# Identity and norm vectors loaded ahead of x, three chunks of x turned ahead of the first q tile, first two V quads queued among the q tiles

## The chip, the cores and the metric

The kernel runs on one core of a Trainium2 chip, written directly for its engines: TensorE (PE) multiplies and transposes, VectorE (DVE), ScalarE (ACT) and GpSimd (POOL) work on what it leaves, SyncE (SP) issues all the DMAs. Each engine runs its own list of instructions in order and waits on semaphores. The metric is the device time of one execution in microseconds, lower is better; the median of several runs is compared.

## The reference

One inference step of a one-layer decoder, all in float32. Prompt: 256 tokens; sample: 8 sequences of 4 new tokens, each with 2048 past tokens in a paged K/V pool (pages of 128 tokens).

```
h = rmsnorm(x, norm1_g)                      # x: 256 + 32 rows of 2048
q, k, v, u = split(h @ w_in)                 # w_in: 2048 x 4096
a = moba_attention(q, k, v, cache_k, cache_v, page_table)  # 8 heads of 128, top 3 blocks of 256
p = pool_mixer(u, hist)                      # causal means over 2, 4, 8, 16 tokens, then w_pool
x = x + concat(a, p) @ w_out
h2 = rmsnorm(x, norm2_g)
x = x + (silu(h2 @ w_gate) * (h2 @ w_up)) @ w_down         # width 5632
y = rmsnorm(x, norm_f_g)
```

Outputs are y, the new K and V rows and the pooling history.

## The kernel before

All 288 rows of x are held transposed: xT is 16 chunks of 128 features by 288 tokens. To come near float32 accuracy with the faster matmul format, every weight and every activation is split into a high and a low part. ACT writes the high part (w_hi at L576, hh at L579), DVE the low part (w_lo at L838, hl at L843), and PE adds three products (L1412, L1413, L1414).

**Weights** come as tiles of 128 x 1024 floats (512 KB). SP's `load` (L405) puts a tile into one of four raw slots; from the fifth on it first waits until PE has used the tile four before it. ACT makes w_hi, DVE w_lo in place, PE's `w_tile` (L1403) uses it. The first 16 tiles give q (q tiles 0 to 15: four 128-column blocks by two chunks by three products, 24 matmuls each), the next 48 (kvu tiles) give u, v and k.

**Start.** SP issues the tables (identity, ones, masks and biases, one DMA of 641 KB), x (two of 1 MB, one of 256 KB), four vectors (norm gains and pool scale) into `vec`, the page table, then q tiles 0 to 3 and `hist` (L397 to L460). PE waits for the tables and all four vectors, turns `vec` into gains (L1423), waits for x, and turns the chunks of x, each with three transposes (`x_turned`, L1426; helper `turn`, L1418) into one of three PSUM banks. DVE copies each chunk out (`x_taken`, L867, copy at L869). X_AHEAD = 6 chunks are turned and copied before anything else; then for each q tile j of the first eight PE turns chunks 2j + 6 and 2j + 7, waits until hl of chunks 2j and 2j + 1 is there, and does the tile. ACT (L604) and DVE (L884) follow the same order: two hh, one w_hi, two squares; two hl, one w_lo, two copies. Before q tile 8 PE adds the squares with `ones` from the tables (`sum_sq`, L1434) and waits for the mean.

**SP's order among the q tiles** (L457 to L465): the load of tile k, for k = 6 to 13 one K page after it (eight pages, the first two quads of K). Then kvu tiles 0 to 3, then load_v(0) and load_v(1), each four pages of V of 512 KB into one of two V buffers (L432), then kvu tiles 4 and 5, then the loop over the 32 quads: four K pages, four V pages, two or so kvu tiles a step. A page's number is read from `pages` into a register (L419) before its DMA is issued (L423 for K, L441 for V). load_v(0) waits until all of x and hist are transposed, as the V buffers lie over xs, vec and hist. load_v(n) from n = 2 waits until PE has used quad n - 2.

**After the q tiles** DVE turns the first K quad (L880) between w_lo of q tile 15 and w_lo of kvu tile 0. PE does kvu tiles 0 and 1, replicates q (L1470), then alternates K logits (L1525), kvu tiles and V products (L1507). V quad 0 is first read there in the second sequence's turn, near 147 us. Then come prompt attention, w_out, and from about 640 us the feed-forward loop.

Of the kernel before, what the change touches and what calls it, by code (L numbers as in the profile page):

```python
# [29 lines left out]
P = 128  # L30
# [38 lines left out]

OA_ORDER = (2, 3, 0, 1)  # L70
NORM2_ORDER = tuple(range(8, 16)) + tuple(range(8))
X_AHEAD = 6

K_BLOCKS = [(a, b) for b in range(T // 32) for a in range(4)]

# [74 lines left out]
def tile_at(k, i=0, per=0):  # L150

    if k < T_FF:
        return k, k // RAW, k % RAW, k % HI
    m = k - T_FF
    s = m % RAW_FF
    earlier = T_FF // RAW if s < RAW else 0
    return k + per * i, earlier + m // RAW_FF + (per // RAW_FF) * i, s, k % HI
# [12 lines left out]
def step_program(nc, A, O, at):  # L170
    ctx = ExitStack()
    with ctx:
        def sem(name):
            return ctx.enter_context(nc.semaphore(name))

        def sb(name, shape, dt=F32, stack=None):
            return (stack or ctx).enter_context(nc.sbuf_tensor(name, shape, dt))


        tab = sb("tab", [P, at["rel"][0]])  # L180
# [39 lines left out]
        rel = ext[:, :, :, :].rearrange("p c b i -> p (c b i)")[:, 0:384]  # L220
# [36 lines left out]
        vec = sb("vec", [56, P], stack=pre)  # L257
# [50 lines left out]
        tab_in, x_in, vec_in, pages_in = sem("tab_in"), sem("x_in"), sem("vec_in"), sem("pages_in")  # L308
# [46 lines left out]
        def final_step(n):  # L355
            part = n // 4
            return part, n % 4, P if part < 2 else TS
# [36 lines left out]
        @block.sync  # L394
        def _(sp):
            xp, xsam = A["x_prompt"][0], A["x_sample"].rearrange("b q d -> (b q) d")
            sp.dma_start(tab[:, :], A["tables"][:, 0:at["rel"][0]]).then_inc(tab_in, 16)  # L397
            for n in range(2):
                sp.dma_start(xs[:, n, :], xp[n * P:(n + 1) * P, :]).then_inc(x_in, 16)
            sp.dma_start(xs[0:TS, 2, :], xsam).then_inc(x_in, 16)  # L400
            for n, name in enumerate(("norm1_g", "norm2_g", "norm_f_g", "pool_scale")):
                g = A[name] if name == "norm_f_g" else A[name][0]
                sp.dma_start(vec[16 * n:min(16 * n + 16, 56), :], g.rearrange("(c p) -> c p", p=P)).then_inc(vec_in, 16)

            def load(t, src, free=True):  # L405

                _, _, s, _ = t
                if free:
                    sp.wait_ge(w_used, slot_free(t))
                k, w = src.shape[0] // P, src.shape[1]  # L410
                sp.dma_start(w_raw[:, s, 0:k * w].rearrange("p (k n) -> p k n", k=k),  # L411
                             src.rearrange("(k p) n -> p k n", p=P)).then_inc(w_in_s[s], 16)
# [4 lines left out]
            def page(pool, b, n):  # L417
                e = NPAGES * b + n
                idx = sp.value_load(pages[0:1, bass.ds(e, 1)], min_val=0, max_val=pool.shape[0] - 1)  # L419
                return pool[bass.ds(idx, 1), :, :].rearrange("a t n -> (a t) n")  # L420

            def load_k_page(n, g):
                sp.dma_start(kpage[:, n % 2, g, :], page(ck, n // NQUADS, 4 * (n % NQUADS) + g)  # L423
                             ).then_inc(k_in[n % 2][g], 16)
# [7 lines left out]
            def load_v(n):  # L432

                if n >= 2:
                    sp.wait_ge(v_done, n - 1)
                elif n == 0:

                    sp.wait_ge(xT_in, KC)
                    sp.wait_ge(hist_T, 2)
                for g in range(4):  # L440
                    sp.dma_start(vpage[:, n % 2, g, :], page(cv, n // NQUADS, 4 * (n % NQUADS) + g)  # L441
                                 ).then_inc(v_in[n % 2], 16)
# [9 lines left out]
            def load_kvu(n):  # L452
                m, r = n // 4, n % 4
                c0 = 4 * AW - CW * (m + 1)
                load(tile_at(T_KVU + n), w_in_d[512 * r:512 * r + 512, c0:c0 + CW])

            for k in range(16):  # L457
                c, j = k // 8, k % 8
                if k == 4:
                    sp.dma_start(hist[:, :], A["state_pool"][0].rearrange("b i c -> (b i) c")).then_inc(hist_in, 16)  # L460
                load(tile_at(T_Q + k), w_in_d[256 * j:256 * j + 256, 512 * c:512 * c + 512], free=k >= RAW)
                if k == 6:
                    sp.wait_ge(pages_in, 16)
                if 6 <= k < 14:
                    load_k_page((k - 6) // 4, (k - 6) % 4)  # L465
            for k in range(4):
                load_kvu(k)
            load_v(0)
            load_v(1)
            load_kvu(4)  # L470
            load_kvu(5)
            kp, vp = O["k_prompt"][0, 0].rearrange("t h d -> t (h d)"), O["v_prompt"][0, 0]
# [358 lines left out]
        def _(dve):  # L831
# [3 lines left out]
            def lo(t):  # L835
                n, _, s, u = t
                dve.wait_ge(hi_ready, n + 1)
                V.tensor_tensor(w_lo[:, s, :], w_raw[:, s, :], w_hi[:, u, :].bitcast(F32),  # L838
                                ALU.subtract).then_inc(lo_ready, 1)
# [27 lines left out]
            def x_taken(c):  # L867
                dve.wait_ge(xT_in, c + 1)
                V.tensor_copy(xT[:, c, :], XB[c % 3][:, 0:T]).then_inc(x_ready, 1)  # L869
# [11 lines left out]

            for c in range(X_AHEAD):
                x_taken(c)
            for j in range(8):  # L884
                for c in (2 * j, 2 * j + 1):
                    gained_lo(0, c, c)
                lo(tile_at(j))
                for c in (2 * j + X_AHEAD, 2 * j + X_AHEAD + 1):
                    if c < KC:
# [510 lines left out]
        def _(pe):  # L1400
            PE = nc.tensor

            def w_tile(t, width, chunks, banks, xh, xl, start, stop):  # L1403

                n, _, s, u = t
                pe.wait_ge(lo_ready, n + 1)
                for m, out in enumerate(banks):
                    for i, c in enumerate(chunks):
                        a = width * i + P * m
                        wh, wl = w_hi[:, u, a:a + P], w_lo[:, s, a:a + P]  # L1410
                        o = out[:, 0:T]
                        PE.matmul(o, wh, xh[:, c, :], start=start and i == 0, stop=False)  # L1412
                        PE.matmul(o, wh, xl[:, c, :], start=False, stop=False)  # L1413
                        last = PE.matmul(o, wl, xh[:, c, :], start=False, stop=stop and i == len(chunks) - 1)  # L1414
                last.then_inc(w_used, 1)

            def turn(out, in_, rows):
                return PE.transpose(out, in_, ident[0:rows, 0:rows])  # L1418
# [7 lines left out]
            def x_turned(c):  # L1426
                if c >= 3:
                    pe.wait_ge(x_ready, c - 2)
                for n in range(3):
                    rows = P if n < 2 else TS  # L1430
                    last = turn(XB[c % 3][:, P * n:P * n + rows], xs[0:rows, n, P * c:P * c + P], rows)
                last.then_inc(xT_in, 1)

            def sum_sq(stage):  # L1434
                pe.wait_ge(sq_added, KC * stage + KC)
                PE.matmul(bank[7][:, 0:T], ones, ssq[:, :], start=True, stop=True).then_inc(sq_summed, 1)

            for c in range(X_AHEAD):
                x_turned(c)

            for k in range(16):
                c, j = k // 8, k % 8
                if c == 0:
                    for n in (2 * j + X_AHEAD, 2 * j + X_AHEAD + 1):
                        if n < KC:
                            x_turned(n)
                    pe.wait_ge(h_ready, 2 * j + 2)
                if k in (2, 5):

                    n = k // 5  # L1450
                    pe.wait_ge(hist_in, 16)
                    pe.wait_ge(*((gains_ready, 1), (ext_ready, 1))[n])
                    for m in range(4):
                        last = turn(bank[6][:, 120 * m:120 * m + 120], hist[:, 512 * n + P * m:512 * n + P * m + P],
                                    NB * HIST)
                    last.then_inc(hist_T, 1)
                if k == 8:

                    pe.wait_ge(ext_ready, 2)
                    sum_sq(0)  # L1460
                    pe.wait_ge(ms_ready, 1)
                w_tile(tile_at(k), 512, (2 * j, 2 * j + 1), bank[4 * c:4 * c + 4], hh, hl, j == 0, j == 7)
# [278 lines left out]
            for k in range(16):  # L1741
                c, j = k // 4, k % 4
# [12 lines left out]
            for j in range(8):  # L1755
                pe.wait_ge(h_ready, KC + 2 * j + 2)
                c = NORM2_ORDER[2 * j]
# [36 lines left out]
            for n in range(12):  # L1794
                part, c, rows = final_step(n)
# [42 lines left out]
```

## Time and profile before

| | |
|---|---|
| median of 3 runs | 1486.53 us (1486.39 to 1490.85) |
| profiled execution, its own time | 1484.65 us |
| its span, first to last instruction | 1482.9 us |
| PE busy | 1400.8 us (94%) |
| DVE busy | 902.4 us (61%) |
| ACT busy | 501.9 us (34%) |
| HBM read | 328.10 MB, 225 GB/s over the span |
| mean granted TensorE clock | 0.986 of full |

Times in the trace are microseconds from the first instruction. "Busy" of PE counts the time in which a matmul is in flight, so its matmuls overlap and their durations are about twice their pitch. SPq, PEq and so on are the engines' queues, where DMAs are issued. A bracket such as "[1.32 <-DVE ms L848]" tells how long the engine stood before it and whose result ended the wait.

### The profile page before, as it was taken

Reading aid. Unit: us, or ns where it says so; the run is one execution under the profiler, and the core shown is the slowest. Engines: PE = TensorE matmul, PEld = TensorE weight load, DVE = VectorE, ACT = ScalarE, POOL = GpSimd, SP = SyncE. Lnnn points to the kernel's source line nnn. Section 1 sums busy time; section 2 is a strip of 40 time slices with the busy share of each in tenths; the row PEclk is TensorE's granted clock in tenths of the full one; section 3 lists DMA queues with packets and bytes.
Section 4 is the critical chain, followed back from the end, with each engine's and each line's share of the span. In section 5 each row is a group of like instructions: output and inputs, shape, how many; then the busy total and the mean of one; then the engine's idle time right before and its main releaser. Section 6 shows DMA issues by size and latency. Waiting matters only on the chain.

```text
span 1482.9 us, 34088 instructions
## 1 busy us (share of the span) xinstructions
PE 1400.8 (94%) x13894; PEld 1298.0 (88%) x13894; DVE 902.4 (61%) x1352; ACT 501.9 (34%) x663; POOL 109.3 (7%) x184
## 2 busy tenths in 40 slices
PE   6998999998688999999999999999999999999986
PEld 5987777776455789999999999999999999999986
DVE  4678777767666645787554555545554646464635
ACT  4322122112123333544343434343333333333333
POOL 2127500000001000200000000000000000000003
PEclk9999999999899999999999999999999999999998
DMA  5798999999999665655555555555555555555531
GB/s 187 257 327 292 371 401 400 399 399 392 404 369 328 219 205 177 199 158 192 175 162 168 168 160 166 170 164 162 169 166 161 168 169 160 166 170 164 164 126 65
DMA packets 164280, 334.41 MB, mean 226 GB/s; under 512 B 10223, under 2 KB 54440, under 8 KB 163599
## 3 DMA queue, kind: packets, MB, share of 16 engines
q1 hardware_dynamic: 164183, 333.06, 66.3%
q8 instruction: 68, 1.11, 0.3%
q14 instruction: 29, 0.24, 0.0%
HBM read 328.10 MB, written 5.27 MB: 225 GB/s over the span
## 4 chain that ended last, share of the span: by engine, by line
PE 78%; SPq 9%; DVE 5%; DMA 3%; issue 3%; ACT 1%; POOL 0%; POOLq 0%; ACTq 0%; DVEq 0%
PE banks L1412 23%; PE banks L1413 23%; PE banks L1414 23%; PE banks L1525 3%; SPq L419 3%; SPq L423 3%; SPq L441 2%; DVE kpage L880 2%; PE banks L1507 2%; DMA vpage<-in_cache_v 2%; PE banks L1418 2%; SPq L411 1%; DMA vec<-in_pool_scale 1%; DMA w_raw<-in_w_out 1%; PE banks L1591 0%
## 5 line engine op out<-in xcount | busy, mean ns | idle before, releaser
L838 DVE TENSOR_TENSOR w_lo<-w_raw,w_hi 128x1024 fp32r<-128x1024 f32 x360 | 440.3, 1229 | 416.2 <-ACT w_hi L576 415.2
L1412 PE MATMUL banks<-hh,w_hi 128*128 128x288 f32 x2176 | 645.7, 297 | 5.3 <-DVE w_lo L838 1.5
L1413 PE MATMUL banks<-hl,w_hi 128*128 128x288 f32 x2176 | 644.3, 296 | 0.0
L1414 PE MATMUL banks<-hh,w_lo 128*128 128x288 f32 x2176 | 642.0, 295 | 0.8 <-issue 0.8
L576 ACT ACTIVATE w_hi<-w_raw 128x1024 fp32r<-128x1024 f32 x360 | 378.9, 1058 | 687.1 <-PE banks L1414 462.2
L1412 PEld LDWEIGHTS banks<-hh,w_hi 128*128 128x128 f32 x2176 | 410.3, 189 | 23.4 <-issue 17.3
L1413 PEld LDWEIGHTS banks<-hl,w_hi 128*128 128x128 f32 x2176 | 410.5, 189 | 1.1 <-issue 1.0
L1414 PEld LDWEIGHTS banks<-hh,w_lo 128*128 128x128 f32 x2176 | 409.5, 188 | 0.6 <-issue 0.6
L1412 PE MATMUL banks<-ah,w_hi 128*128 128x288 f32 x704 | 208.8, 297 | 9.5 <-DVE af L1252 5.4
L1414 PE MATMUL banks<-ah,w_lo 128*128 128x288 f32 x704 | 209.5, 298 | 0.0
L1413 PE MATMUL banks<-al,w_hi 128*128 128x288 f32 x704 | 209.2, 297 | 0.0
L880 DVE STREAM_TRANSPOSE kpage<-kpage 128x1024 f32<-128x1024 f32 x128 | 150.1, 1217 | 13.5 <-DMA kpage<-in_cache_k 12.9
L1412 PEld LDWEIGHTS banks<-ah,w_hi 128*128 128x128 f32 x704 | 134.4, 191 | 10.0 <-issue 5.6
L1413 PEld LDWEIGHTS banks<-al,w_hi 128*128 128x128 f32 x704 | 134.4, 191 | 0.0
L1414 PEld LDWEIGHTS banks<-ah,w_lo 128*128 128x128 f32 x704 | 134.0, 190 | 0.0
L1525 PE MATMUL banks<-kpage,qr 32*32 32x256 f32 x4096 | 94.5, 407 | 17.3 <-DVE kpage L880 13.1
L1525 PEld LDWEIGHTS banks<-kpage,qr 32*32 32x32 f32 x4096 | 60.9, 106 | 45.2 <-DVE kpage L880 17.6
L1507 PE MATMUL banks<-vpage,pT 128*32 128x512 f32 x512 | 65.1, 621 | 12.8 <-DMA vpage<-in_cache_v 11.3
L1344 POOL COPY ssq<-sq 128x288 f32<-128x288 f32 x3 | 1.7, 551 | 939.2 <-ACT sq L593 939.2
L1207 DVE TENSOR_TENSOR xT<-xT,banks 128x288 f32<-128x288 f32 x176 | 67.8, 447 | 0.0
L1507 PEld LDWEIGHTS banks<-vpage,pT 128*32 128x32 f32 x512 | 17.3, 142 | 43.1 <-issue 29.9
L1347 POOL TENSOR_TENSOR ssq<-ssq,sq 128x288 f32<-128x288 f32 x45 | 43.2, 960 | 53.4 <-ACT sq L593 48.8
(193 smaller groups left out, 646.4 us busy)
## 6 DMA issues: line engine op xcount, KB each, us to landing
kpage<-in_cache_k SPq DMA_DIRECT2D x128, 512.0 KB, 7.9
vpage<-in_cache_v SPq DMA_DIRECT2D x128, 512.0 KB, 7.0
w_raw<-in_w_gate SPq DMA_DIRECT2D x88, 512.0 KB, 3.6
w_raw<-in_w_up SPq DMA_DIRECT2D x88, 512.0 KB, 3.6
w_raw<-in_w_down SPq DMA_DIRECT2D x88, 512.0 KB, 3.6
w_raw<-in_w_in SPq DMA_DIRECT2D x64, 512.0 KB, 9.7
w_raw<-in_w_out SPq DMA_DIRECT2D x32, 512.0 KB, 4.0
xs<-in_x_prompt SPq DMA_DIRECT2D x2, 1024.0 KB, 7.4
```

Of the source, the lines that this page charges most:

```text
L419: idx = sp.value_load(pages[0:1, bass.ds(e, 1)], min_val=0, max_val=pool.shape[0] - 1)
L423: sp.dma_start(kpage[:, n % 2, g, :], page(ck, n // NQUADS, 4 * (n % NQUADS) + g)).then_inc(k_in[n % 2][g], 16)
L576: return nc.scalar.activation(out, in_, ACT.Copy)
L838: V.tensor_tensor(w_lo[:, s, :], w_raw[:, s, :], w_hi[:, u, :].bitcast(F32), ALU.subtract).then_inc(lo_ready, 1)
L880: V.transpose(kpage[:, n % 2, g, :], kpage[:, n % 2, g, :]).then_inc(k_turned, 1)
L1207: ins = V.tensor_tensor(xT[:, m0 + m, :], xT[:, m0 + m, :], bank[4 * quad + m][:, 0:T], ALU.add)
L1347: G.tensor_tensor(ssq[:, :], ssq[:, :], sq[:, c % 2, :], ALU.add).then_inc(sq_added, 1)
L1412: PE.matmul(o, wh, xh[:, c, :], start=start and i == 0, stop=False)
L1413: PE.matmul(o, wh, xl[:, c, :], start=False, stop=False)
L1414: last = PE.matmul(o, wl, xh[:, c, :], start=False, stop=stop and i == len(chunks) - 1)
L1507: last = PE.matmul(OB[x][32 * g:32 * g + 32, :], pT[:, g, bass.ds(j, 32, 4)], vpage[:, n % 2, g, 512 * x:512 * x + 512], start=j == 0, sto ...
L1525: last = PE.matmul(S[32 * x:32 * x + 32, a, :], qr[32 * a:32 * a + 32, at_:at_ + 32], keys, start=j == 0 and c == 0, stop=j == NQUADS - 1 ...
```

## The change

The tables are loaded in two pieces: the identity alone first, the rest after the load of q tile 1, with its own count on the same semaphore, for which PE waits before q tile 8. The four vectors are issued right after the identity, before x. X_AHEAD goes from 6 to 3 for PE and DVE; PE then turns chunks 2j + 3 and 2j + 4 before q tile j, for j to 6, and DVE copies them after w_lo of tile j. load_v(0) moves to behind the load and K page of k = 11, load_v(1) to behind those of k = 13.

```diff
-X_AHEAD = 6
+X_AHEAD = 3
...
-            sp.dma_start(tab[:, :], A["tables"][:, 0:at["rel"][0]]).then_inc(tab_in, 16)
+            sp.dma_start(tab[:, 0:P], A["tables"][:, 0:P]).then_inc(tab_in, 16)
+            for n, name in enumerate(("norm1_g", "norm2_g", "norm_f_g", "pool_scale")):
+                g = A[name] if name == "norm_f_g" else A[name][0]
+                sp.dma_start(vec[16 * n:min(16 * n + 16, 56), :], g.rearrange("(c p) -> c p", p=P)).then_inc(vec_in, 16)
             for n in range(2):
                 sp.dma_start(xs[:, n, :], xp[n * P:(n + 1) * P, :]).then_inc(x_in, 16)
             sp.dma_start(xs[0:TS, 2, :], xsam).then_inc(x_in, 16)
-            for n, name in enumerate(("norm1_g", "norm2_g", "norm_f_g", "pool_scale")):
-                g = A[name] if name == "norm_f_g" else A[name][0]
-                sp.dma_start(vec[16 * n:min(16 * n + 16, 56), :], g.rearrange("(c p) -> c p", p=P)).then_inc(vec_in, 16)
...
             for k in range(16):
                 c, j = k // 8, k % 8
+                if k == 2:
+                    sp.dma_start(tab[:, P:at["rel"][0]], A["tables"][:, P:at["rel"][0]]).then_inc(tab_in, 16)
                 if k == 4:
                     sp.dma_start(hist[:, :], A["state_pool"][0].rearrange("b i c -> (b i) c")).then_inc(hist_in, 16)
                 load(tile_at(T_Q + k), w_in_d[256 * j:256 * j + 256, 512 * c:512 * c + 512], free=k >= RAW)
...
                 if 6 <= k < 14:
                     load_k_page((k - 6) // 4, (k - 6) % 4)
+                if k in (11, 13):
+                    load_v((k - 11) // 2)
             for k in range(4):
                 load_kvu(k)
-            load_v(0)
-            load_v(1)
             load_kvu(4)
             load_kvu(5)
...
                 if k == 8:
 
                     pe.wait_ge(ext_ready, 2)
+                    pe.wait_ge(tab_in, 32)
                     sum_sq(0)
                     pe.wait_ge(ms_ready, 1)
```

## Rows read from the trace of the kernel before

**Rows 1.** The page, part 4: the chain that ended last, by engine.
```profile
PE 78%; SPq 9%; DVE 5%; DMA 3%; issue 3%; ACT 1%; POOL 0%; POOLq 0%; ACTq 0%; DVEq 0%
```

**Rows 2.** Windows: stretch, us, PE, PEld, DVE, ACT, POOL busy, PEclk, DMA share, GB/s.
```profile
55.00:70.00 15.00, 14.38 (x109) 14.39 (x109) 10.47 (x15) 4.87 (x7) 0.00 (x0) 1.00 0.78 264
70.00:82.00 12.00, 12.00 (x93) 12.00 (x92) 9.71 (x10) 4.31 (x5) 0.00 (x0) 1.00 0.54 170
...
100.00:120.00 20.00, 19.57 (x389) 17.08 (x388) 15.57 (x16) 5.32 (x6) 17.08 (x37) 1.00 1.02 369
120.00:155.00 35.00, 30.41 (x535) 25.37 (x518) 33.56 (x53) 8.83 (x10) 27.50 (x59) 1.00 0.80 273
155.00:400.00 245.00, 218.99 (x3682) 168.18 (x3680) 173.65 (x270) 43.08 (x56) 13.28 (x31) 0.98 1.04 400
```

**Rows 3.** The chain of waits from 0 to 60: start us, us, what.
```profile
4.25 8.15 DMA vec<-in_pool_scale
...
12.53 5.50 PE banks L1418 x19
18.05 0.46 DVE xT L869
...
19.90 1.15 DVE w_lo L838
...
24.40 0.24 PE banks L1412
...
25.26 0.14 PE banks L1414
...
47.46 5.39 DMA w_raw<-in_w_in
```

**Rows 4.** The tile xs (x as loaded), its DMAs.
```profile
DMA to landing us min/median/max: 6.1/8.6/9.7
```

**Rows 5.** Timeline from 0: start us, us, engine, line, operation.
```profile
2.12 0.66 SPq L400 DMA_DIRECT2D xs<-in_x_sample  x1
2.82 0.92 SPq L403 DMA_DIRECT2D vec<-in_norm_g  x2
...
14.36 1.28 ACT L579 ACT_TABLE_LOAD   x1 [14.36 <-DVE xT L869]
```

**Rows 6.** Timeline of SP's queue, 52 to 99.
```profile
53.84 0.37 SPq L411 DMA_DIRECT2D w_raw<-in_w_in  x1
...
59.08 0.37 SPq L411 DMA_DIRECT2D w_raw<-in_w_in  x1
...
82.51 8.08 SPq L441 DMA_DIRECT2D vpage<-in_cache_v  x8
90.64 0.99 SPq L411 DMA_DIRECT2D w_raw<-in_w_in  x2
```

**Rows 7.** Timeline of ACT: w_hi of q tile 11 and of kvu tile 4.
```profile
58.47 1.06 ACT L576 ACTIVATE w_hi<-w_raw 128x1024 fp32r<-128x1024 f32 x1 [1.48 <-DMA w_raw<-in_w_in]
...
98.95 1.06 ACT L576 ACTIVATE w_hi<-w_raw 128x1024 fp32r<-128x1024 f32 x1 [12.86 <-DMA w_raw<-in_w_in]
```

**Rows 8.** Timeline of DVE: w_lo of q tile 15, K turns, w_lo of kvu tiles 0, 1.
```profile
73.51 1.23 DVE L838 TENSOR_TENSOR w_lo<-w_raw,w_hi 128x1024 fp32r<-128x1024 f32 x1 [1.25 <-ACT w_hi L576]
74.65 4.62 DVE L880 STREAM_TRANSPOSE kpage<-kpage 128x1024 f32<-128x1024 f32 x4
79.19 2.32 DVE L838 TENSOR_TENSOR w_lo<-w_raw,w_hi 128x1024 fp32r<-128x1024 f32 x2
```

**Rows 9.** Timeline of PE: q tile 8's first matmul, and replicate_q.
```profile
55.62 0.40 PE L1412 MATMUL banks<-hh,w_hi 128*128 128x288 f32 x1 [1.32 <-DVE ms L848]
...
87.45 1.89 PE L1470 MATMUL banks<-z,sq 128*128 128x256 f32 x8
```

**Rows 10.** A long PE pause: windows as rows 2, then the timeline row that ends it.
```profile
380.00:383.00 3.00, 0.00 (x0) 0.00 (x0) 2.86 (x11) 0.00 (x0) 0.00 (x0) 1.00 1.03 414
383.00:386.00 3.00, 0.00 (x0) 0.00 (x0) 3.00 (x4) 0.00 (x0) 0.00 (x0) 0.52 1.02 419
...
386.31 3.65 PE L1507 MATMUL banks<-vpage,pT 128*32 128x512 f32 x16 [6.42 <-DMA vpage<-in_cache_v]
```

## The prediction

> **What bounds the kernel now.** I read the chain of waits by engine first, to see who sets the end: PE has 78% of it, SP's queue (SPq) 9%, DMA 3% [rows 1]. Then busy time by stretch, to see where PE is not the limit [rows 2]: from 155 to 400 us the DMA engines are busy all the time (share 1.04, 400 GB/s), so there the transfers set the pace; between 55 and 82 us they have room (shares 0.78 and 0.54). A megabyte moved into that room is free only if nothing urgent is queued behind it.
>
> The chain of the first 60 us shows the places that the change touches [rows 3]. PE starts at 12.53, released by the last norm vector (issued 4.25, 8.15 us to land). The chain goes through 19 transposes (5.50 us), a DVE copy, two hl, w_lo at 19.90, and the first q matmul at 21.2. It is PE from there to 47.46, then the landing of one q weight tile (5.39 us) and its conversions. The first matmul of q tile 8 is at 55.62, and replicate_q, which follows kvu tiles 0 and 1, at 87.45 [rows 9]. Ten tiles in 31.8 us are 3.18 us each: PE has no pause in this stretch, so every microsecond by which a weight tile is late there is a microsecond of the kernel.
>
> **Part 1: identity and vectors ahead of x.** Now x_sample, issued at 2.12, lands at most 9.7 us later, at 11.8 [rows 4, 5], and the vectors at 12.4 [rows 3]. That a 4 KB vector takes 8.15 us shows that the queue serves in order: it lands behind the 3.0 MB (641 KB of tables, 2.3 MB of x) before it. The change takes 577 KB from in front of x: 577 KB at 0.35 to 0.40 MB/us is 1.4 to 1.6 us. It puts four vector issues there, of 0.37 to 0.49 us each (2.82 to 4.62 in all, 1.8 us). x so lands at 11.4 to 12.1, against a start of 12.53: a gain of 0.4 to 1.1, and I take 0.6. The rest of the tables goes behind q tile 1's load, 40 us before its first reader at k = 8; the added wait on it costs nothing. It delays the loads of q tiles 2 and 3 by 1.5 us, whose conversions start 5 us after those of tiles 0 and 1.
>
> **Part 2: three chunks ahead.** After: PE turns 3 + 2 chunks before q tile 0, not 6 + 2, but it was never PE that ended this; DVE copied six chunks first, the last at 18.05 [rows 3]. With three, the chain goes over ACT: chunk 0 copied, table load (1.28 us, at 14.36 now [rows 5]), two hh, w_hi, then w_lo. From the rows: w_hi would end at 17.56 and w_lo 1.2 later at 18.8, so q tile 0 starts 2.3 us earlier than 21.18. Before tile 5 ends, PE must turn two chunks more than now between the tiles (10, not 8, at 0.47 us): 0.94 back. That leaves 1.3, and with part 1 1.9 us. TensorE's clock may take some: matmuls run at a pitch of 0.24 us (1.2 GHz) to 24.6 and at 0.13 (2.4 GHz) from there [rows 3]. If the rise moves along with tile 0, nothing is lost; if it stays at its time, 2.3 us more of matmuls run at half pace, 1.15 us lost. I take 0.4 lost: part 1 and 2 together gain 1.5 us. Bounds: 2.6 gained (x at 11.4, rise moves along), or 1.5 lost, where the shorter lead makes PE wait (third rival). The gain reaches q tile 8: load 9 waits for tile 5, and the 8.2 us from there to tile 8 stay.
>
> **Part 3: eight V pages among the q tiles.** What is removed: eight V loads at 82.51 to 90.59, in front of kvu tiles 4 and 5 (90.64) [rows 6]. What is added: the same 4.2 MB, four pages after k = 11's K page and four after k = 13's, each 1.1 us of SP's time (a register load, then the issue). The wait in load_v(0), on xT_in and hist_T, has long been met. SP's own lateness is small: q tile 12 issued at 59.8 instead of 59.08, tile 14 at 68.3 instead of 65.4. The queue behind matters more.
>
> Count from q tile 11: issued 53.84, converted from 58.47 [rows 6, 7]; its data ended about 1.1 us before that, at 57.3. In the new order behind it stand: K page 5, four V, q tile 12, K, q tile 13, K, four V, q tile 14: fourteen loads of 512 KB (0.524 MB). At which rate? With work always queued the windows show 369 GB/s (100 to 120 us) and 400 (155 to 400) [rows 2]. And the one row that shows a weight load behind eight V pages: kvu tile 4, issued at 90.64, converted at 98.95 [rows 6, 7], that is nine loads in about 14.2 us, 0.33 MB/us. I take 0.37, nearest to the stretch next to this one: 1.42 us a load. Fourteen take 19.9 us: tile 14 ends at 77.2, lands at 78.3, and is converted (w_hi 1.06, w_lo 1.2) at 80.7. PE, with tile 13 done at about 75.8 (tile 12 late by one microsecond for the same reason), waits some 5 us. Tile 15 lands at 79.7, its w_lo ends at 82.0, where now it ends at 74.7. Behind it on DVE stand the four K turns (4.62) and w_lo of kvu tile 0, which ends at 80.4 now [rows 8] just before PE wants it at 80.9, so at 87.8 then. PE's side says the same: tile 14 at 80.7, two tiles of 3.18, and a slow clock after the pause. After a PE pause of 6.4 us the granted clock stood at 0.52 of full [rows 10]; 3.4 us at half pace, as many as shown slow in tile 0, are 1.7 lost: 88.8. Kvu tile 0 so starts 7 to 8 us late. I take 7.3. At 400 GB/s and no clock loss it is 5.3; at 0.33 and with the loss 10.
>
> The Trainium skill (TensorE: Matmul & The Clock Gate, "HAM oscillation — how this bites in real kernels") speaks against the change in the same place: waits of PE for a DMA throttle the clock, so that the next work starts slow. The rows at 383 to 386 agree [rows 10]; by that rule the stall costs its length and then some 1.7 us, without it the sum would be lower by about 0.7, as DVE's chain hides the rest.
>
> **Does the delay stay?** Nothing behind it waits with slack. From 87 to 120 us PE is the limit. With V gone from 82 to 91, kvu tiles 4 to 7 and the K pages land earlier, but kvu tile 4's w_lo waited for PE anyway; I give 0.3 us for it. From 120 to 155 DVE and PE alternate and the DMA share is 0.80 [rows 2]: the engines are ahead of their buffers there, because each next K and V load waits for PE to release its buffer. So the transfer-bound stretch begins when PE gets there, with the same bytes left: it starts and ends late by the same amount, and the PE-bound rest follows.
>
> Sum: -1.5 + 7.3 - 0.3 = +5.5 us. On the profiled execution (1484.65 with a span of 1482.9) this is 1490.2. The median of the runs is 1486.53, 1.9 above it; on this the forecast is 1492.0. That is +0.37%; 0.3%, 4.5 us, is what a measurement can tell from no change, so the slower verdict is near its edge.
>
> **Rivals.**
> 1. Not slower: the weight tiles do not fall behind the V pages. Mechanism: SP puts the pages in while the engines have room (0.78 and 0.54 between 55 and 82 us), they are served beside the others, and q tile 14 lands in time. PE wants it converted at 74.5, so landed at 72.1. For it: between 55 and 82 us some 6.0 MB move in 27 us, capacity 10. Against: 14 loads by 71.0 from 57.3 need 0.54 MB/us, which no window shows; and the vector's 8.15 us. It decides from the point where tile 14 lands by 72.1. Price: only the start is left, -1.5: 1485.0. Chance 0.20.
> 2. The V bytes are repaid: 4.2 MB less after 82 us let a transfer-bound stretch begin earlier; were all from 85 to 400 us bound by transfers, 4.2 MB at 400 GB/s would be 10.5 us: +5.8 - 10.5, 1481.8. For it: shares of 1.02 at 100 to 120. Against: 0.80 at 120 to 155. Chance 0.08.
> 3. The shorter lead starves PE: a chunk is turned one tile before its use. From its transpose to w_lo: two copies 1.0, two hl 1.1 to 1.9, w_lo 1.2, in all 3.3 to 4.1, and ext's copy 0.65 in two tiles, against 4.6 us of PE work (0.47 + 3.18 + 0.94). DVE would be late by up to 0.5 in six tiles: 3 us lost, so +8.5, 1495.0. Chance 0.10.
>
> The forecast has 0.62; its own range is 1489.5 to 1495 (start gain 0 to 2.6, stall 5.3 to 9). The range for 8 in 10: 1486.5 to 1496. Chances: slower takes 0.43 of the forecast and the third rival, 0.53. Within 0.3%: 0.19 of the forecast and the first rival, 0.39. Faster: the second, 0.08.
>
> **What would show it.** Right: the first transpose near 12.0; q tile 0 near 18.5; w_hi of q tile 12 onward late and PE idle 4 to 6 us before tile 14, released by w_lo behind a landing of w_raw; a granted clock near 0.5 after it; replicate_q some 5 to 6 us later than 87.45; the 400 GB/s stretch as long as before and shifted. Wrong: no PE pause between q tiles 12 and 15 (first rival); the transfer-bound stretch ending earlier than its start moved (second); pauses before tiles 2 to 7 with DVE as releaser (third).

## The result, and the profile after

| | before | after |
|---|---|---|
| median of 10 runs each, us | 1487.55 (1484.11 to 1491.98) | 1494.97 (1490.97 to 1497.2) |
| ratio, 95% interval | | 1.0049 (1.0036 to 1.0062) |
| span of the profiled execution | 1482.9 | 1493.2 |
| its own time | 1484.65 | 1495.01 |
| mean granted TensorE clock | 0.986 | 0.977 |

The changed kernel is 7.4 us slower. (Of the later measurements the ratios leave out two executions that took several times as long as the others, 4709.24 us of the kernel before and 5609.22 of e3.) Its lines are two or three higher than before (w_hi L578, w_lo L840, products L1414 to L1416, logits L1528).

The chain of waits of the changed kernel, from 0 to 130 us (start, us, what). At the start the last landing that PE waits for is now that of x, not that of a norm vector. Later, from 53.03 to 67.18, the chain goes over SP's issues of K, V and weight loads, and then over the load of q tile 14, which the chain of before did not have; it had the load at 47.46 [rows 3].

```profile
3.85 8.30 DMA xs<-in_x_sample
12.19 0.94 PE banks L1420 x3
...
13.77 1.28 ACT L581
...
17.01 1.23 DVE w_lo L840
...
18.38 0.58 PE banks L1414
...
67.18 9.89 DMA w_raw<-in_w_in
77.09 1.06 ACT w_hi L578
78.18 1.24 DVE w_lo L840
79.46 0.40 PE banks L1414
```

SP's timeline, after. The eight V issues of [rows 6] now stand between the loads of q tiles 11 and 12 (53.03, 59.51) and before that of tile 14 (67.18):

```profile
53.03 0.37 SPq L411 DMA_DIRECT2D w_raw<-in_w_in  x1
54.15 0.36 SPq L423 DMA_DIRECT2D kpage<-in_cache_k  x1
55.35 4.12 SPq L441 DMA_DIRECT2D vpage<-in_cache_v  x4
59.51 0.43 SPq L411 DMA_DIRECT2D w_raw<-in_w_in  x1
...
63.54 3.60 SPq L441 DMA_DIRECT2D vpage<-in_cache_v  x4
67.18 27.18 SPq L411 DMA_DIRECT2D w_raw<-in_w_in  x8
```

ACT's timeline, after: w_hi of q tiles 11, 12, 13 and 14. The brackets are the idle time before each, and all four were ended by a landing of weights. Before, tile 11's was 1.48 us [rows 7]:

```profile
57.62 1.06 ACT L578 ACTIVATE w_hi<-w_raw 128x1024 fp32r<-128x1024 f32 x1 [2.22 <-DMA w_raw<-in_w_in]
...
66.75 1.06 ACT L578 ACTIVATE w_hi<-w_raw 128x1024 fp32r<-128x1024 f32 x1 [8.07 <-DMA w_raw<-in_w_in]
...
69.56 1.06 ACT L578 ACTIVATE w_hi<-w_raw 128x1024 fp32r<-128x1024 f32 x1 [1.75 <-DMA w_raw<-in_w_in]
...
77.09 1.06 ACT L578 ACTIVATE w_hi<-w_raw 128x1024 fp32r<-128x1024 f32 x1 [6.48 <-DMA w_raw<-in_w_in]
```

PE's timeline, after: the first matmuls of q tiles 8, 12 and 14, then replicate_q. The two middle rows are pauses that the kernel before does not have [rows 9]:

```profile
54.03 0.40 PE L1414 MATMUL banks<-hh,w_hi 128*128 128x288 f32 x1 [0.55 <-DVE ms L850]
...
69.12 0.40 PE L1414 MATMUL banks<-hh,w_hi 128*128 128x288 f32 x1 [2.08 <-DVE w_lo L840]
...
79.46 0.40 PE L1414 MATMUL banks<-hh,w_hi 128*128 128x288 f32 x1 [2.18 <-DVE w_lo L840]
...
93.80 1.89 PE L1473 MATMUL banks<-z,sq 128*128 128x256 f32 x8
```

Windows, after, columns as in [rows 2]. PE's busy time falls by 1.46 and 2.18 us in the first two stretches, while the DMA share rises from 0.78 to 0.99 and from 0.54 to 0.85; the clock is at half behind each pause (0.50 and 0.51, that is 1.2 of 2.4 GHz). In the room left by V, 82 to 95, the DMA engines stand more than half idle. The last stretch is bound by transfers at the rate of before, 400 GB/s:

```profile
55.00:70.00 15.00, 12.92 (x97) 12.69 (x96) 8.17 (x12) 2.97 (x4) 0.00 (x0) 0.99 0.99 370
70.00:82.00 12.00, 9.82 (x56) 9.59 (x56) 4.91 (x5) 4.44 (x5) 0.00 (x0) 0.78 0.85 317
...
70.00:73.00 3.00, 3.00 (x14) 3.00 (x14) 1.23 (x1) 0.61 (x1) 0.00 (x0) 0.50 1.02 416
80.00:83.00 3.00, 3.00 (x15) 3.00 (x15) 3.00 (x4) 2.02 (x2) 0.00 (x0) 0.51 0.13 44
...
82.00:95.00 13.00, 13.00 (x91) 12.87 (x91) 8.20 (x12) 2.78 (x4) 0.00 (x0) 0.94 0.41 122
...
165.00:400.00 235.00, 216.12 (x3627) 165.06 (x3617) 166.33 (x253) 41.89 (x53) 13.21 (x30) 0.98 1.04 400
```

### The profile page after: what moved, and what is told of

Its sections match the earlier page's. It is cut to its first block, busy times and chain, and to the rows that moved or that the text cites. A ratio compares the mean times of both kernels' runs of the same rounds, so it can differ in the third digit from the quotient of the medians.

```text
span 1493.2 us, 34089 instructions
## 1 busy us (share of the span) xinstructions
PE 1410.0 (94%) x13894; PEld 1305.6 (87%) x13894; DVE 899.9 (60%) x1352; ACT 501.0 (34%) x663; POOL 114.3 (8%) x184
## 4 chain that ended last, share of the span: by engine, by line
PE 77%; SPq 10%; DMA 4%; DVE 3%; issue 3%; ACT 1%; POOL 0%; POOLq 0%; ACTq 0%; DVEq 0%
PE banks L1414 23%; PE banks L1415 23%; PE banks L1416 23%; SPq L419 4%; PE banks L1528 3%; SPq L423 3%; SPq L441 2%; DMA vpage<-in_cache_v 2%; PE banks L1510 2%; PE banks L1420 2%; DVE kpage L882 1%; SPq L411 1%; DMA w_raw<-in_w_in 1%; DMA w_raw<-in_w_out 1%; DMA xs<-in_x_sample 1%
## 5 line engine op out<-in xcount | busy, mean ns | idle before, releaser
L840 DVE TENSOR_TENSOR w_lo<-w_raw,w_hi 128x1024 fp32r<-128x1024 f32 x360 | 439.8, 1228 | 421.3 <-ACT w_hi L578 420.1
L1414 PE MATMUL banks<-hh,w_hi 128*128 128x288 f32 x2176 | 648.9, 298 | 9.2 <-DVE w_lo L840 6.4
L1416 PE MATMUL banks<-hh,w_lo 128*128 128x288 f32 x2176 | 644.6, 296 | 1.1 <-issue 1.1
L578 ACT ACTIVATE w_hi<-w_raw 128x1024 fp32r<-128x1024 f32 x360 | 378.6, 1058 | 676.9 <-PE banks L1416 461.0
L1414 PEld LDWEIGHTS banks<-hh,w_hi 128*128 128x128 f32 x2176 | 413.1, 190 | 28.6 <-issue 18.6
L1416 PEld LDWEIGHTS banks<-hh,w_lo 128*128 128x128 f32 x2176 | 412.0, 189 | 0.5 <-issue 0.5
L1414 PE MATMUL banks<-ah,w_hi 128*128 128x288 f32 x704 | 208.7, 296 | 9.5 <-DVE af L1254 5.4
L1416 PE MATMUL banks<-ah,w_lo 128*128 128x288 f32 x704 | 209.4, 297 | 0.0
L1414 PEld LDWEIGHTS banks<-ah,w_hi 128*128 128x128 f32 x704 | 134.2, 191 | 9.9 <-issue 5.6
L1416 PEld LDWEIGHTS banks<-ah,w_lo 128*128 128x128 f32 x704 | 133.9, 190 | 0.0
L1528 PE MATMUL banks<-kpage,qr 32*32 32x256 f32 x4096 | 95.0, 411 | 13.3 <-DVE kpage L882 9.9
L1528 PEld LDWEIGHTS banks<-kpage,qr 32*32 32x32 f32 x4096 | 61.2, 106 | 42.6 <-issue 14.9
L1510 PE MATMUL banks<-vpage,pT 128*32 128x512 f32 x512 | 66.3, 631 | 14.1 <-DMA vpage<-in_cache_v 12.9
L1349 POOL TENSOR_TENSOR ssq<-ssq,sq 128x288 f32<-128x288 f32 x45 | 47.6, 1059 | 53.9 <-ACT sq L595 49.6
```

Source lines behind the costliest of these rows:

```text
L578: return nc.scalar.activation(out, in_, ACT.Copy)
L1349: G.tensor_tensor(ssq[:, :], ssq[:, :], sq[:, c % 2, :], ALU.add).then_inc(sq_added, 1)
L1510: last = PE.matmul(OB[x][32 * g:32 * g + 32, :], pT[:, g, bass.ds(j, 32, 4)], vpage[:, n % 2, g, 512 * x:512 * x + 512], start=j == 0, sto ...
L1528: last = PE.matmul(S[32 * x:32 * x + 32, a, :], qr[32 * a:32 * a + 32, at_:at_ + 32], keys, start=j == 0 and c == 0, stop=j == NQUADS - 1 ...
```

## The experiments

To follow a gain or a loss from stage to stage I read four events in every trace: q tile 8's first matmul, DVE's first copy of the replicated q, the reduction that closes batch 1 of the paged attention, and the first silu of the feed-forward part. Times in us; the last two columns are the span and the median, with the ratio to the kernel before on the same chip. Every row is a single profile; those marked "again" are a second profile of the same kernel.

| kernel | q tile 8 | q copied | batch 1 | silu | span | median (ratio) |
|---|---|---|---|---|---|---|
| before | 55.62 | 89.38 | 169.85 | 645.51 | 1482.9 | 1487.55 |
| before, again | 55.61 | 89.37 | 171.26 | 647.82 | 1485.8 | |
| after | 54.03 | 95.72 | 178.76 | 655.49 | 1493.2 | 1494.97 (1.0049) |
| after, again | 54.56 | 97.18 | 178.95 | 653.45 | 1491.5 | |
| V move only | 54.84 | 97.98 | 181.62 | 657.92 | 1496.1 | 1495.79 (1.005) |
| start parts only | 54.88 | 88.64 | 170.29 | 647.61 | 1485.0 | 1487.1 (1.0) |
| V's first 64 columns early | 53.92 | 88.80 | 169.82 | 645.60 | 1483.4 | 1489.84 (1.0016) |
| V one by one | 54.93 | 89.76 | 170.46 | 646.42 | 1484.6 | 1487.65 (1.0004) |
| one V quad early | 54.22 | 89.89 | 172.17 | 648.92 | 1486.8 | 1491.31 (1.0021) |
| one V quad, again | 54.76 | 90.63 | 173.92 | 649.91 | 1488.2 | |
| K earlier, V early | 54.20 | 91.26 | 173.18 | 651.87 | 1489.9 | 1491.55 (1.0024) |
| X_AHEAD = 3 only | 54.96 | 88.73 | 171.79 | 647.67 | 1485.2 | 1487.76 (0.9999) |
| first loads' order only | 54.35 | 88.12 | 168.68 | 646.83 | 1485.2 | 1486.73 (0.9991) |
| K earlier, four chunks ahead | 52.66 | 86.42 | 171.10 | 647.90 | 1485.7 | 1485.45 (0.9986) |

**e1, the V move by itself**, in the kernel before:

```diff
                 if 6 <= k < 14:
                     load_k_page((k - 6) // 4, (k - 6) % 4)
+                if k in (11, 13):
+                    load_v((k - 11) // 2)
             for k in range(4):
                 load_kvu(k)
-            load_v(0)
-            load_v(1)
             load_kvu(4)
```

> The kernel before with part 3 alone (both V quads among the q tiles). My theory, weight tiles queued behind the V pages: PE pauses 4 to 6 us before q tile 14 and replicate_q begins 7 to 9 us later than 87.45; the time is 8 to 10 us above before. The rival that the loss comes from the start (shorter lead, new order of the first loads): no change from before, within 1 us.

Measured: 1495.79 against 1487.39, ratio 1.005 (1.0036 to 1.0063). PE's timeline of this kernel, q tiles 12 and 14:

```profile
69.89 0.40 PE L1412 MATMUL banks<-hh,w_hi 128*128 128x288 f32 x1 [2.09 <-DVE w_lo L838]
...
80.50 0.61 PE L1412 MATMUL banks<-hh,w_hi 128*128 128x288 f32 x1 [4.00 <-DVE w_lo L838]
```

The V move alone carries the whole slowdown, with pauses in the same two places. Q tile 8 started at 54.84 here, 0.8 earlier than in both profiles of before, although nothing of its start was changed. So 0.8 us at tile 8, in a single profile, can be the difference of two executions.

**e2, the start parts by themselves**: the changed kernel with V back in its old place.

```diff
-                if k in (11, 13):
-                    load_v((k - 11) // 2)
             for k in range(4):
                 load_kvu(k)
+            load_v(0)
+            load_v(1)
```

> Parts 1 and 2 alone, V back in its old place. My theory: q tile 0 starts 2.8 us earlier as in the trace after, replicate_q 1 to 2 us earlier than 87.45, the time 1 to 2 us below before. The rival that the shorter lead starves PE: slower than before by up to 3 us.

Measured: 1487.1 against 1487.39, ratio 1.0 (0.9991 to 1.001). DVE copied q at 88.64, 0.73 earlier than in the kernel before (table), but at batch 1 and at the end nothing of it can be told from the spread. I had expected 1 to 2 us less; the interval goes from 1.3 us faster to 1.5 slower, so a gain of 1 us is neither shown nor excluded.

**e3, the same V issues with few bytes**: in the changed kernel each early page brings 64 of its 1024 columns, the other 960 come where V was loaded before.

```diff
                 if k in (11, 13):
-                    load_v((k - 11) // 2)
+                    load_v_cols((k - 11) // 2, 0, 64, v_pre)
             for k in range(4):
                 load_kvu(k)
+            load_v_cols(0, 64, AW, v_in[0])
+            load_v_cols(1, 64, AW, v_in[1])
```

> The changed kernel, but the eight early V loads carry only 64 of 1024 columns each (32 KB, not 512), and the other 960 columns come at the old place, so that SP spends the same time in the same places. If the bytes in the queue cause the loss (my theory), PE has no pause over 1 us among q tiles 12 to 15 and the time is that of parts 1 and 2 alone, plus up to 1 us for eight more issues later. If SP's late issue of q tile 14's load causes it (it came 2 us late), the pause stays, 3 us or more, and the time stays 5 us or more above before.

Measured: 1489.84 against 1487.39, ratio 1.0016 (1.0007 to 1.0025). PE's timeline, q tiles 12 and 14:

```profile
70.41 0.40 PE L1422 MATMUL banks<-hh,w_hi 128*128 128x288 f32 x1 [0.30 <-DVE w_lo L848]
...
80.42 0.40 PE L1422 MATMUL banks<-hh,w_hi 128*128 128x288 f32 x1 [0.23 <-DVE w_lo L848]
```

SP was the other suspect, as the chain of the changed kernel goes over its issues. Here it spends as long on the eight issues (4.09 and 3.59 us for 4.12 and 3.60) and issues q tile 14's load at 66.77 for 67.18, yet the pauses shrink from 2.08 and 2.18 us to 0.30 and 0.23: the bytes in the queue make them, not SP's time. Its median is 2.7 over e2's (2.3 without the one long execution), more than the up to 1 us expected, while its profile shows nothing lost (span 1483.4, q copied at 88.80); that profile was the fastest of its executions. Where the median's excess comes from, I can't say. So e3 shows what makes the pauses, and not that all of the 7.4 us is theirs.

**e4, V early but one page at a time**: the start parts, and one V page behind each load from q tile 14 to kvu tile 5.

```diff
+                if k >= 14:
+                    load_v_page(k - 14)
-            for k in range(4):
-                load_kvu(k)
-            load_v(0)
-            load_v(1)
-            load_kvu(4)
-            load_kvu(5)
+            for k in range(6):
+                load_kvu(k)
+                load_v_page(k + 2)
```

> Parts 1 and 2, with one V page behind each weight load from q tile 14 to kvu tile 5, in place of two blocks of four. Between 70 and 82 us the DMA engines were 0.54 busy. My theory: one page more per 3.2 us step is served in time, PE has no pause over 1 us, time as parts 1 and 2 alone or up to 1 us less, as kvu tiles 4 and 5 and the K pages come sooner. If early V is harmful wherever it stands, the time is 3 us or more above parts 1 and 2 alone.

Measured: 1487.65 against 1487.39, ratio 1.0004 (0.9995 to 1.0013); one PE pause of 0.79 us, before kvu tile 0 at 81.37. As many bytes, issued between 66.3 and 89.5 us, cost nothing when they stand one behind each weight tile. This changes two things at once: the pages are spread, and the first is issued 11 us later than in the changed kernel (66.31 for 55.35). Which of the two does it was not tried. They bring nothing either: e4 ends where e2 does.

**e5, one V quad early**: the start parts, load_v(0) behind k = 11, load_v(1) in its old place.

```diff
-                if k in (11, 13):
-                    load_v((k - 11) // 2)
+                if k == 11:
+                    load_v(0)
             for k in range(4):
                 load_kvu(k)
+            load_v(1)
```

> Parts 1 and 2, load_v(0) after k = 11 as in the change, load_v(1) in its old place. Queue theory: six loads (K, four V, q tile 12) stand where two did, so q tile 12 is converted 1 to 2 us late and PE pauses up to 1.5 us there, but q tile 14 has only K pages and q tiles behind the four V pages, ten loads by 14.2 us, and is in time within 1 us. The time is 0 to 2 us above parts 1 and 2 alone (1487.1). If any V block among the q tiles costs the same, it is half of the loss, 4 us.

Measured: 1491.31 against 1487.59, ratio 1.0021 (1.0009 to 1.0034), above the 0 to 2 us that I had expected. The pause before tile 12 is there (1.56 us at 68.74), tile 14 is in time. Four pages cost about half of what eight do, 3.7 us over before. The profile shows 1.9 of it at batch 1 (172.17 against 170.29), a second one 3.6 (173.92, e11).

**e6, more room behind the K pages**: in the changed kernel K pages 0 to 3 are loaded ahead of q tile 3 and the other four behind tiles 4 to 7; V stays early.

```diff
-                if k == 6:
+                if k == 3:
                     sp.wait_ge(pages_in, 16)
-                if 6 <= k < 14:
-                    load_k_page((k - 6) // 4, (k - 6) % 4)
+                    for g in range(4):
+                        load_k_page(0, g)
+                if 4 <= k < 8:
+                    load_k_page(1, k - 4)
```

> The changed kernel, with K pages 0 to 3 ahead of q tile 3's load (at 6 us, into the time before 27 us in which the DMA engines stood) and K pages 4 to 7 behind q tiles 4 to 7. Of the fourteen loads up to q tile 14 eleven are left, so by the queue theory it lands three loads, 4 us, sooner: the pause before it shrinks from some 4 us to 0 to 1 us and the time falls to 1 to 4 us above before. If it is not the bytes in the queue (a bank, the V buffers), the pause and the 7.4 us stay.

Measured: 1491.55 against 1487.59, ratio 1.0024 (1.0013 to 1.0035). PE's timeline, q tiles 12 and 14:

```profile
67.62 0.40 PE L1416 MATMUL banks<-hh,w_hi 128*128 128x288 f32 x1 [0.46 <-DVE w_lo L842]
...
75.86 0.40 PE L1416 MATMUL banks<-hh,w_hi 128*128 128x288 f32 x1 [1.63 <-DVE w_lo L842]
```

With three K pages fewer between load 11 and load 14, both pauses shrink and about half of the loss goes: what stands in front of the weight tile counts. The pause before tile 14 is longer than the 0 to 1 us expected, and the 4.0 us over before are at the upper edge of what I had expected.

**e7, X_AHEAD by itself**, in the kernel before:

```diff
-X_AHEAD = 6
+X_AHEAD = 3
```

> The kernel before with X_AHEAD = 3 alone. My theory: q tile 0 starts 2 us earlier than 21.18, but PE then turns two chunks more between the tiles, and the wait for the mean before q tile 8 ends 0.5 to 1 us earlier than 55.1; the time is within 1.5 us of before. Rival, starved PE: q tile 8 later than before.

Measured: 1487.76 against 1487.59, ratio 0.9999 (0.9989 to 1.001). Q tile 0 started at 18.77, 2.4 us earlier than before, tile 8 at 54.96, 0.66 earlier, which is no more than e1 came early with no change there.

**e8, the order of the first loads by itself**: the start parts with X_AHEAD back at 6.

```diff
-X_AHEAD = 3
+X_AHEAD = 6
```

> The kernel before with the new order of the first loads alone (identity and vectors ahead of x, rest of the tables behind q tile 1), six chunks ahead. My theory: the first transpose of x at 12.2 instead of 12.8, everything after it 0.3 to 0.6 us earlier, the time within 1 us of before. If the small vector loads hold up x, it starts later than 12.8.

Measured: 1486.73 against 1487.59, ratio 0.9991 (0.9979 to 1.0002). First transpose at 12.02, q tile 0 at 20.43, tile 8 at 54.35, 1.27 earlier. The first transpose of x began at 11.63 to 12.41 in the ten profiles with the new order (12.06 on average) and at 12.26 to 12.93 in the four with the old one (12.64), so the order is worth some 0.6 us there.

**e9 to e11, three kernels looked at once more**, unchanged: before, after, and one V quad early, to see how much of a difference between two profiles is a difference between two executions.

> The kernel before once more, for a second profile. In the first one the 128 K logits after the 2.9 us pause at 131.6 took 2.76 us (full clock); in all nine profiles of other kernels they took 3.8 to 4.5. If the clock there falls by chance of the moment, this profile shows either; if a changed start brings it about, it shows 2.76 again. The copy of the replicated q (89.38) comes within 1 us of that.

> The changed kernel once more. Both pauses before q tiles 12 and 14 come again with 1.5 to 3 us each, and the copy of the replicated q (95.72) within 1.5 us of that; the later half-clock logits may or may not come.

> One V quad early, once more: its timed median was 3.7 us above before, its first profile showed only a pause of 1.6 us before q tile 12 and own time 1488.7. If the early block costs more in most executions than in the profiled one, this profile shows a longer pause at q tile 12 or another one at 13 to 15, and replicated q later than 89.9 by 1 to 3 us; if the difference lies behind that, replicated q is at 89 to 90 again.

PE's timeline of after, again (tiles 12 and 14), and of one V quad early, again (tile 12):

```profile
68.95 0.40 PE L1414 MATMUL banks<-hh,w_hi 128*128 128x288 f32 x1 [1.38 <-DVE w_lo L840]
...
80.11 0.61 PE L1414 MATMUL banks<-hh,w_hi 128*128 128x288 f32 x1 [4.10 <-DVE w_lo L840]
```

```profile
69.13 0.40 PE L1415 MATMUL banks<-hh,w_hi 128*128 128x288 f32 x1 [1.41 <-DVE w_lo L841]
```

The pauses come back in the same places with other lengths; I had expected 1.5 to 3 us for each, and they took 1.38 and 4.10. Of e11, q was copied at 90.63, between the two outcomes that it was to decide (89 to 90, or 1 to 3 us later than 89.9). Before came out 2.9 us longer in its span (1485.8) than the first time. At q tile 8 and at the copy of q its two profiles agree within 0.01 us. The first logits after the pause near 131 us, in which PE waits for DVE, took 1.76 us longer in the second; 1.4 us of this are left at batch 1. PE's timeline of the first profile of before, then of the second:

```profile
131.63 2.76 PE L1525 MATMUL banks<-kpage,qr 32*32 32x256 f32 x128 [2.90 <-DVE kpage L880]
```

```profile
131.60 4.52 PE L1525 MATMUL banks<-kpage,qr 32*32 32x256 f32 x128 [3.08 <-DVE kpage L880]
```

The first profile of before kept the full clock through this pause. In each of the thirteen others these logits took 3.80 to 4.53 us, the unchanged kernel's second profile among them, so no changed start is needed for it. In the first of the changed kernel:

```profile
139.23 4.53 PE L1528 MATMUL banks<-kpage,qr 32*32 32x256 f32 x128 [3.68 <-DVE kpage L882]
```

So the 10.3 us between the first two spans hold a difference that the change did not make. The four pairs of a profile of before and one of after differ by 5.7, 7.4, 8.6 and 10.3 us; the medians say 7.4. Below I compare with the second profile of before, whose logits near 131 are as slow as those of the changed kernel.

**e12, a version that could beat both**: new order of the first loads, X_AHEAD = 4, K pages as in e6, V in its old place.

```diff
-X_AHEAD = 3
+X_AHEAD = 4
...
-                if k in (11, 13):
-                    load_v((k - 11) // 2)
...
             for k in range(4):
                 load_kvu(k)
+            load_v(0)
+            load_v(1)
```

> A try for a faster version: new order of the first loads, four chunks ahead, K pages 0 to 7 early as in the run before with them, both V quads at their old place. q tile 8 no longer waits for a load behind K pages, so it starts 1 to 1.5 us earlier than in the kernel before (55.6); nothing else changes: 1 to 1.5 us below before, at the edge of what can be told. If the end of the first stage does not carry over to the end of the kernel, no change.

Measured: 1485.45 against 1487.93, ratio 0.9986 (0.9976 to 0.9997): 2.5 us faster than the kernel before (2.1 by the ratio, 0.4 to 3.6 by the interval). It is the only faster version whose interval excludes no change, and the interval nearly touches it. I had expected tile 8 earlier by 1 to 1.5 us; it came 2.95 earlier than in the second profile of before, and so did the copy of q (86.42), but batch 1 at 171.10 only 0.16 earlier. Windows of the stretch in which the first half of the lead goes, of e12 and then of the second profile of before, each with the first logits:

```profile
86.00:95.00 9.00, 7.21 (x150) 5.59 (x149) 8.32 (x9) 0.00 (x0) 0.00 (x0) 0.81 1.03 394
...
88.17 3.63 PE L1530 MATMUL banks<-kpage,qr 32*32 32x256 f32 x128 [1.79 <-DVE qr L933]
```

```profile
86.00:95.00 9.00, 7.21 (x158) 5.85 (x157) 5.59 (x7) 0.32 (x1) 0.00 (x0) 1.00 0.98 380
...
91.13 2.75 PE L1525 MATMUL banks<-kpage,qr 32*32 32x256 f32 x128 [1.79 <-DVE qr L929]
```

The clock takes 1.5 us: DVE has the result of the kvu tile behind these logits 12.59 us after the copy of q, for 11.10. The other 1.25 us up to the logits near 131, which take 4.52 us in both, go mostly into the same two places as in the first profile of the changed kernel: a longer stop of PE inside a kvu tile (0.89 us at 112.66 for 0.24 at 113.45) and three small DVE operations before the K pages (1.54 us for 0.80). Why these vary is open. So is which of the three edits the gain comes from.

## Why the prediction was right, point by point

It forecast 1492.0 and slower, by 5.5 us; measured were 1494.97 and 7.4. The mechanism was the one named; the sizes of its three terms were off. By the medians, the V move alone cost 8.4 us (e1) where stall and relief had been put at 7.0, and the start parts alone gave 0.3 (e2) where they had been put at 1.5. The sizes in the profiles were these.

**Part 1 and 2, the start: -1.5 forecast, about -1 at tile 8, nothing that can be told at the end.** x ended PE's wait at 12.19 (11.63 the second time) for 12.53 before, forecast 12.0 from a 0.6 gain; q tile 0 came at 18.38, forecast 18.5. At tile 8, 1.59 was left in the first profile of after, 1.06 in the second, 0.74 in e2, and e1 was 0.8 early without any of it. The 8.2 us from load 9 to tile 8 did stay (45.80 to 54.03), but not for the reason given: load 9 is no longer the last to arrive. The wait before ms is now ended by PE itself, with its tiles 6 and 7, last chunks and sum; that this takes as long is luck. The prediction also read wrongly that it was never PE that ended the six chunks before q tile 0: the chain has 19 transposes of PE there [rows 3], and DVE's copies waited for each chunk. The forecast for tile 0 held all the same. DVE's timeline, after, at ms:

```profile
53.52 0.46 DVE L850 TENSOR_SCALAR ms<-banks 128x288 f32<-128x288 f32 x1 [0.58 <-PE banks L1438]
```

Of the two cases for the pitch of the first matmuls each came once. Full pitch began at 24.8 us before, with tile 0 at 21.18. In the first profile of after it moved along, to 22.1, with tile 0 at 18.38. In the second it stayed, at 25.1, with tile 0 at 17.82. The term of 0.4 us lost was an average over the two. That this is the clock is not shown by the profile's own figure: the granted clock reads 1.00 from 22 to 24 us in the first profile of before, at a pitch of 0.24.

**Part 3, the stall: +7.3 forecast, +7.9 and +8.9 in the two profiles.** From q tile 8 to replicate_q are 39.8 us where they were 31.8 (54.03 to 93.80, [rows 9]). The fourteen loads from tile 11 (landed at 57.6) to tile 14 (77.07) took 19.5 us, 1.39 each or 0.377 MB/us, where the prediction took 0.37 and had tile 14 land at 78.3. It was converted at 79.4, forecast 80.7. What differed is the shape: I had one wait of 5 us before tile 14 and one microsecond before tile 12. The trace has 2.08 and 2.18, and half the clock behind both, for some 3.3 us each, which is 1.6 lost each: 2.1 + 2.2 + 3.2 = 7.5 of the 7.9. The second time the pauses were 1.38, 0.17 and 4.10, near the forecast, with the full clock behind the first. Behind the last, matmuls ran at a pitch of 0.24 us until 85.3, which is 2.3 lost: 7.95 of the 8.9, the rest not placed. Replicate_q began 6.35 us later than before, in the second profile 7.8, where 5 to 6 had been named as the sign.

The rule of the Trainium skill that the prediction weighed (TensorE: Matmul & The Clock Gate, "HAM oscillation — how this bites in real kernels": waits for a DMA throttle the clock and the next work starts slow) went the right way, and the trace agrees, with the windows above: a clock of 0.51 from 80 to 83, behind the pause of 2.18 us before tile 14. It does not hold for every such wait here: in e1 a pause of 2.09 us before tile 12 left the clock at 1.00. The row from 383 to 386 that the prediction read as the clock after a pause [rows 10] lies inside the pause (PE x0); the four microseconds behind it read 0.51 as well.

That the loads wait for each other was shown from both sides. e3 keeps the issues and takes the bytes: pauses of 0.30 and 0.23 us are left. e4 keeps the bytes and spreads them: one of 0.79 us. e5 and e6 shorten the line: about half the loss each. The one result that does not fit is e3's median, some 2 us over e2's without a pause that would account for it. The Trainium skill (DMA: Bandwidth & Descriptors, "Queues, rings and completion order") has it that each DMA engine takes the descriptors of a ring, its part of one queue, in ring order; the load of tile 14, 9.89 us from issue to landing behind V pages, against the 5.39 of [rows 3], agrees.

**The relief of 0.3: not seen.** The first profile of after against the second of before has the loss grow between the copy of q and batch 1, from 6.35 us (95.72 against 89.37) to 7.5 (178.76 against 171.26). The second profile of after has it go from 7.8 to 7.7. The growth in the first is two small delays. One is a stop of PE inside a kvu tile, 0.89 us for 0.24 before; it was 0.77 in the second profile. The other is three small DVE operations before the K pages, 1.55 us for 0.80 before and 0.63 in the second profile. The stop in the first profile of after, then the longest of the three operations in it and in the second profile of before:

```profile
120.45 0.29 PE L1416 MATMUL banks<-hh,w_lo 128*128 128x288 f32 x1 [0.89 <-issue]
...
133.42 0.69 DVE L950 SCALAR_TENSOR_TENSOR d<-d,tab 128x2 f32<-128x2 f32 x1
...
126.41 0.26 DVE L948 SCALAR_TENSOR_TENSOR d<-d,tab 128x2 f32<-128x2 f32 x1
```

The logits near 131 to 139 take the same in both (4.53 and 4.52). What makes the delays come and go is not known. From batch 1 on the distance stays in the first profile of after, 7.7 at silu and 7.4 at the end, as the prediction said; in the second it falls from 7.7 to 5.6 at silu and 5.7 at the end. From batch 1 to silu the fourteen profiles took 474.5 to 478.7 us, so single profiles don't decide this; the medians do, with 7.4 at the end.

**The rivals.** The first, weights not late, is refuted by the pauses. The second, V's bytes repaid, by the windows: from 82 to 95 the DMA share is 0.41, where the engines could have run ahead, and 165 to 400 goes on at 400 GB/s with a share of 1.04; e4, which moves the same bytes without a pause, gains nothing over e2. The third, PE starved by the shorter lead, by e7: 2.4 us earlier at tile 0 and no slower at the end; neither there nor in the changed kernel does PE wait between q tiles 0 and 7.

**How close it was.** Of the 3.0 us between 1492.0 and 1494.97, 1.0 is the base: the medians of before measured later (1487.4 to 1487.9) lie 1 us over the 1486.53 known then. The other 1.9 are the difference, forecast too small. The stall was 0.6 to 1.6 longer than forecast, and the start's 1.5 and the relief's 0.3 are not seen in the time. That the stall's size came so close is in part luck: pauses of 1 and 5 us and one slow stretch had been forecast, and in the first profile two pauses of 2 us and two slow stretches added up to nearly the same.

## What to carry to other kernels

An average DMA share of 0.54 or 0.78 does not mean that a block of transfers can be added there: on a queue served in order every load behind the block is late by the block's whole service time (here 1.4 us a 512 KB page), unless its consumer has that much slack. Put such transfers in one at a time behind the urgent ones, which cost nothing here, and ask first whether anybody waits for them: V early, even where it cost nothing, gained nothing. And two single profiles of one kernel differed by 2.9 us in their spans here (1.7 and 1.4 for the two others that were taken twice); take a second profile of each before a term of 1 us is explained.

## What was unexpected of the hardware

- The granted clock after a pause of some 3 us is not a property of the kernel: the same logits of the same program took 2.76 us after a pause of 2.90 and, in another execution, 4.52 after one of 3.08.
- Full pitch at the start came 3.7 us after q tile 0 in one execution of the changed kernel (22.1, tile 0 at 18.38) and 7.3 us after it in another (25.1, tile 0 at 17.82).
- The pause before the first logits is 1.79 us in all fourteen profiles, and the logits behind it took 2.75 us in eleven and 3.63 to 3.95 in three (e6, e7, e12).
- Pauses of one length went either way. Before q tile 12 one of 2.08 us was followed by half clock in the changed kernel's first profile (0.50 from 70 to 73), one of 2.09 in e1 by the full one (windows of e1):

```profile
70.00:71.00 1.00, 1.00 (x8) 1.00 (x9) 0.00 (x0) 0.42 (x1) 0.00 (x0) 1.00 1.03 420
71.00:72.00 1.00, 1.00 (x10) 1.00 (x9) 0.33 (x1) 0.64 (x1) 0.00 (x0) 1.00 1.05 430
```

- The small early V pieces (e3) leave a profile as short as that of before, but a median 2.4 us longer than that of before (2.0 without the one long execution). This stays open.
